# Two half-width subtractions for each low half on GpSimd, and two clears moved to the start of VectorE's program

## What is computed

```
h = rms_norm(x) ; z = h @ w_in                          # first block, 2304 columns
mix = concat(gmlp(z), rglru(z), hgrn2(z), pool(z))       # 256 columns each
x = x + mix @ w_out
x = x + (gelu(conv(hf_gate)) * conv(hf_val)) @ w_down    # hf = rms_norm(x) @ w_up
x = x + (p @ w_pe) * sigmoid(rms_norm(x) @ w_pg)
for l in range(2):                                       # second block
    proj = rms_norm(x) * norm1_g @ w_in
    o_a, o_b, o_c = attention(proj), rwkv7(proj), retention(proj)
    x = x + (g0 * (o_a @ w_attn_o) + g1 * (o_b @ w_rwkv_o) + g2 * (o_c @ w_ret_o)) @ w_out
    x = x + (silu(h2 @ w_ffn_gate) * (h2 @ w_ffn_up)) @ w_ffn_down
```

## Time and profile before

| quantity | value |
|---|---|
| median of three runs | 2712.03 us |
| the profiled execution | 2712.35 us, its span 2710.5 us |
| TensorE (PE) busy | 2621.4 us, 97% of the span |
| VectorE (DVE) busy | 1472.8 us, 54% |
| ScalarE (ACT) busy | 634.3 us, 23% |
| GpSimd (POOL) busy | 1488.5 us, 55% |
| mean granted TensorE clock | 0.992 of full speed |
| DMA, mean over the span | 82 GB/s |

### The profile page before, as it was taken

How to read it: one execution, slowest core, us unless ns; L and a number is a source line. 1 busy time by engine, 2 the same in 40 slices (tenths; PEclk the granted TensorE clock), 3 DMA queues, 4 the chain that set the end, 5 groups by cost and what they waited for, 6 DMA issues and landing times.

```text
span 2710.5 us, 47585 instructions
## 1 busy us (share of the span) xinstructions
PE 2621.4 (97%) x16458; PEld 2043.1 (75%) x16458; DVE 1472.8 (54%) x2059; ACT 634.3 (23%) x1159; POOL 1488.5 (55%) x945
## 2 busy tenths in 40 slices
PE   7889999999999999999999999999999999999999
PEld 5776888877776677787888887766677777888887
DVE  6776737364556637774342424556647774442434
ACT  2333000023324423441200002234413441200002
POOL 4565565655544444456666666644544456666665
PEclk9999999999999999999999999999999999999999
DMA  4212333323211122223333333311122223233332
GB/s 149 67 43 86 93 93 93 93 87 104 85 56 48 36 93 63 59 74 97 93 93 93 93 94 112 94 48 49 41 91 59 71 71 97 93 93 95 95 96 94
DMA packets 72726, 222.67 MB, mean 82 GB/s; under 512 B 9345, under 2 KB 12545, under 8 KB 72577
## 3 DMA queue, kind: packets, MB, share of 16 engines
q1 hardware_dynamic: 72576, 220.63, 27.0%
HBM read 218.50 MB, written 2.10 MB: 81 GB/s over the span
## 4 chain that ended last, share of the span: by engine, by line
PE 88%; DVE 5%; DVEq 2%; issue 2%; DMA 1%; POOL 1%; ACT 1%; POOLq 1%; ACTq 0%; SPq 0%
PE acc L475 77%; PE bank L475 10%; POOL w_lo L354 1%; DMA raw<-in_w_pg 1%; DVEq L1528 1%; PE bank L1048 0%; DVE rw_bon L1086 0%; DVEq L1618 0%; DVE z_rw L1086 0%; DVE rw_SCB L1086 0%; DVE xg_lo L1168 0%; POOL w_hi L347 0%; DMA x<-in_x 0%; DVE rw_Dl L1086 0%; DVE rw_AR L1086 0%
## 5 line engine op out<-in xcount | busy, mean ns | idle before, releaser
L354 POOL TENSOR_TENSOR w_lo<-raw,w_hi 128x1024 fp32r<-128x1024 f32 (+3 forms) x438 | 966.7, 2207 | 303.5 <-PE acc L475 282.3
L347 POOL TENSOR_SCALAR w_hi<-raw 128x1024 fp32r<-128x1024 f32 (+3 forms) x438 | 431.1, 984 | 715.8 <-PE acc L475 607.8
L475 PE MATMUL acc<-xg_hi,w_hi 128*128 128x512 f32 x2224 | 597.5, 406 | 35.7 <-issue 16.2
L475 PE MATMUL acc<-xg_lo,w_hi 128*128 128x512 f32 x2224 | 590.9, 401 | 0.0
L475 PE MATMUL acc<-xg_hi,w_lo 128*128 128x512 f32 x2224 | 588.0, 399 | 0.0
L475 PEld LDWEIGHTS acc<-xg_hi,w_hi 128*128 128x128 f32 x2224 | 414.1, 190 | 153.9 <-issue 60.3
L475 PEld LDWEIGHTS acc<-xg_lo,w_hi 128*128 128x128 f32 x2224 | 418.7, 190 | 105.5 <-issue 5.8
L475 PEld LDWEIGHTS acc<-xg_hi,w_lo 128*128 128x128 f32 x2224 | 416.8, 188 | 101.1 <-issue 0.3
L1895 ACT ACTIVATE ffn_act<-ffn_t 128x512 f32<-128x512 f32 x100 | 63.2, 632 | 778.0 <-DVEq L1146 619.5
L1086 DVE TENSOR_TENSOR x<-x,acc 128x512 f32<-128x512 f32 x104 | 71.3, 689 | 316.1 <-PE acc L475 315.4
L475 PE MATMUL acc<-hid_hi,w_hi 128*128 128x512 f32 x656 | 182.7, 396 | 3.8 <-POOL w_lo L354 1.6
(11 more groups left out here) (342 smaller groups left out, 2835.6 us busy)
## 6 DMA issues: line engine op xcount, KB each, us to landing
raw<-in_w_up SPq DMA_DIRECT2D x132, 512.0 KB, 3.6
raw<-in_w_down SPq DMA_DIRECT2D x48, 512.0 KB, 3.6
raw<-in_w_gate SPq DMA_DIRECT2D x48, 512.0 KB, 3.6
raw<-in_w_ret SPq DMA_DIRECT2D x32, 512.0 KB, 3.6
raw<-in_w_rw SPq DMA_DIRECT2D x28, 512.0 KB, 3.6
raw<-in_w_o SPq DMA_DIRECT2D x48, 256.0 KB, 2.7
raw<-in_w_in SPq DMA_DIRECT2D x18, 512.0 KB, 3.6
raw<-in_w_down SPq DMA_DIRECT2D x24, 384.0 KB, 3.0
```

The lines of the kernel that those rows point to most:

```text
L347: nc.gpsimd.tensor_scalar(w_hi[:, s, 0:n], raw[:, s, 0:n], 1.0, 0.0, ALU.mult, ALU.add).then_inc(w_half[s], 1)
L354: nc.gpsimd.tensor_tensor(w_lo[:, s, 0:n], raw[:, s, 0:n], bits(w_hi[:, s, 0:n]), ALU.subtract).then_inc(w_split[s], 1)
L475: return nc.tensor.matmul(o, a, b, start=first, stop=last, skip_group_check=shared)
```

## The change

Each `low_part` is written as two subtractions of half the columns, one behind the other without a drain between them; the semaphore `w_split` is set by the second. The two clears of VectorE are written ahead of the wait for the first constants (`keep_in`), behind the clear of `sumsq`.

```diff
@@ low_part
-                nc.gpsimd.tensor_tensor(w_lo[:, s, 0:n], raw[:, s, 0:n], bits(w_hi[:, s, 0:n]),
-                                        ALU.subtract).then_inc(w_split[s], 1)
+                for at in (slice(0, n // 2), slice(n // 2, n)):
+                    last = nc.gpsimd.tensor_tensor(w_lo[:, s, at], raw[:, s, at], bits(w_hi[:, s, at]), ALU.subtract)
+                last.then_inc(w_split[s], 1)
@@ start of VectorE's program
             dve.sem_inc(s3["rev"], 1)
             ms(sumsq[:])
+            ms(m1["td"][:])
+            ms(att[:])
             dve.wait_ge(keep_in, load_wait * (len(KEEP) - 1))
@@ behind norm_end(1)
             norm_end(1)
-            ms(m1["td"][:])
-            ms(att[:])
             dve.wait_ge(first_in, load_wait * len(FIRST))
```

## The result

The changed kernel takes 2721.97 us (median of 6 runs, 2716.03 to 2723.58), the kernel before 2712.07 (6 runs beside it, 2710.15 to 2714.28). The ratio is 1.0033, with a 95% interval of 1.0023 to 1.0044. By the bound of 0.2% that is slower, by 9.9 us in the medians and 8.9 us by the ratio. The forecast was 2717.2, and "no change" was given more chance than "slower". The median lies 0.5 us above the upper end of the range (2721.5); by the ratio the time would be 2721.0, and in a second batch the same kernel took 2720.28 (5 runs, ratio 1.0033 again), both just inside it.

The account below looks back on a forecast made before the run. TensorE, busy for 97% of the span, was taken to bound the kernel. Terms of 3.3, 0.75, 0.75, 0.9 and -0.5 summed to +5.2 us, giving 2717.2 us as median; range 2713.0 to 2721.5 us.

Parts of the forecast that it names:

- The price of a subtraction: Every low part on GpSimd: one more subtraction costs 0.15 us, with ends of nothing and 0.35 us.
- Rivals 2 and 4: 2: second half prepared under the first, 2712.6 us, chance 0.12; 4: issue gap between halves, 2724.8 us, chance 0.08.
- Term a: Branch projections and attention part of each layer: TensorE waits for the low part at 22 places, +3.3 us.
- the part on VectorE: Halves reaching TensorE over VectorE: +0.9 us in the recurrence, -0.5 us at 148 us, 0 from 30 to 45 us.
- Term b: Gated embedding: four low parts of slot 0 in a row and one holding up `xg_lo`, +0.75 us.
- Term d: Recurrence, six of eight head pairs: `rw_bon` meets the second half and waits 0.15 us longer, +0.9 us.
- Term e: At 148 us: `m_tc` starts about 0.5 us earlier behind the shorter first half, and this is kept, -0.5 us.
- The zero for 30 to 45 us: First block before TensorE's 4.11 us wait: nothing gained from halves, put at 0, with ends -1 and +0.5 us.
- term c: Four single low parts on the chain and one inside GpSimd's pooling at 172 to 187 us, +0.75 us.
- Rival 1: At `rw_bon` and the convolution: VectorE's waits are halved and this is kept, 2713.0 us, chance 0.15.
- Rival 3: Before 260 us: VectorE's runs pass ahead of GpSimd's second halves, TensorE waits less, 2706.5 us, chance 0.05.

Follow-up runs that it names:

- e6: Kernel before with low parts in quarters everywhere but in the first block's mixers, clears at their old place: 2733.49 us (ratio 1.0081).
- e7: Kernel before with halves only in the layers' attention input pairs and branch projections, clears as before: 2712.97 us (ratio 1.0005).
- e2: Kernel before with halved low parts everywhere, the clears at their old place: 2721.63 us (ratio 1.0030).
- e12: Kernel before with clears moved, halves in first nine input and each layer's first 11 branch pairs, two first-block GpSimd multiplies halved: 2708.55 us (0.9988).
- e9: Kernel before with halves only in the loops that end a layer (output pairs and feed-forward), clears as before: 2710.71 us (ratio 0.9996).
- e4: Kernel before with halved low parts everywhere but in the first block's mixers, clears at their old place: 2717.25 us (ratio 1.0014).

## Why the prediction was right and where it was wrong

**The price of a subtraction** was right: 0.14 us (8.88 for 8.75 in the branch projections, 0.41 for three more in e6), the forecast 0.15. A pair of halves alone took 2.54 to 2.55 us. Rivals 2 and 4 are out by this. (The forecast's own range is a small slip: 38 places by 0.12 to 0.18 us, less 0.5, and one microsecond on either side give 2715.1 to 2719.4, not 2715.3 to 2719.0.)

**Term a, 22 places, +3.3 us**, had the right places and the right price: +1.6 in each layer from 1137 on. What failed is the part on VectorE, which let the change reach TensorE over VectorE only in the recurrence, at 148 and before 45 us. I looked for VectorE's waits where the chain showed them. `an_k` and `an_mx`, 1.70 and 1.20 us in the trace of before, stood in none of my views, and they give 0.9 us back in each layer. With them the 22 places are worth 1.4 us (e7: 0.8).

**Term b, 5 places of the gated embedding, +0.75 us:** the high parts of the circle start at 645.04 and, three rounds on, 667.84 us before, at 644.92 and 668.28 in the changed kernel: 7.79 us for each round instead of 7.60, with 0.15 forecast. The +0.87 of the whole stretch from 575 to 679 us says less, since profiles without a change there have -1.7 to +0.4. Right.

**Term d, `rw_bon`, +0.9 us:** it takes 1.62 us instead of 1.47, as forecast, at the six head pairs named, and from the second head pair to the fourth it is 105.8 us instead of 105.4 in both layers, 0.2 us for each. Right.

**Term e, -0.5 us at 148,** was wrong in sign. I moved `m_tc` against the half of the low part and forgot that GpSimd's next instruction moves too: it was earlier, it was whole, and `m_tc` met it. The zero for 30 to 45 us was too small a gain in most executions: TensorE's wait there, said to grow to 4.4 us, was 1.05 and 1.13 us in the two profiles of the whole change and 3.67 in e2. At 141 us the whole change was 6.7 and 7.4 us ahead, e2 2.2, counted from their first high part. By 250 us nothing of it can be told: -1.3, +0.1 and +2.5 us, where programs unchanged there have -1.8 to +0.1. The part of term c before 250 us lies inside this and was not measured apart.

**What the sum had not at all** is GpSimd's late start at layer 2, 0.9 to 1.3 us once, and the clock: a mean granted clock lower by 0.001 in the medians, with 1 to 3 us. At equal clock the forecast of +5.2 is met by +6 to 8, and in part by luck: a gain of 1.8 in attention, term e's missing 0.5 and the late start nearly cancel. One to three microseconds of the 6 to 8 have no place in this account; the profiles scatter too much between 192 and 1049 us to name one. The clock then took the time to the upper end of the range.

**The rivals.** Rival 1, VectorE's waits shortened and this kept, is what happens in the attention stretch, there with a change of order, and not at `rw_bon`. Rival 3, faster, is what happens up to 141 us: VectorE's run is served ahead of the second halves. I gave it a quarter of 24 us; that much came (6.7 and 7.4 us, not in e2), and was given back at 150 and 188, where GpSimd's own whole instructions and its pooling were next. Its sign, TensorE's waits before 260 us falling by over 5 us together, did not come: 4.11, 3.21 and 2.32 us became 1.05, 6.04 and 6.45. It decided from a point I had not named, whether GpSimd's chain behind is shorter than VectorE's.

## What to carry to other kernels

Splitting an instruction of GpSimd changes when VectorE gets its turn and costs a fixed 0.14 us: split it only where VectorE stands behind it on TensorE's path (here e12's places), and leave it whole where TensorE waits for GpSimd itself. List VectorE's instructions that take longer than their kind by group and form before summing, since the chain of waits shows only the last one. When an engine comes free earlier, ask what it starts next, and read a lead as gained only behind the next place where another engine is late. Before a step between two profiles is put down to a change, look for it in a profile whose program is unchanged up to there.

## What the runs showed of the hardware

- A wait of TensorE can cost more than its length, and not evenly: behind the same 2.35 us wait at the start of the recurrence eight small matmuls took 1.13 us in eight of the profiles and 2.0 in six. Behind the wait at 683 us the half pace lasted 2.1 us longer in the changed kernel and in e9 than in the kernel before, though e9 has the same program there.
- The three series with halves everywhere had a mean granted clock of 0.9902 to 0.9904, the ten others 0.9909 (e4) to 0.9920, over 5 to 11 runs each. Why the whole is lower than its parts stays open.
- GpSimd fetches code at a loop's jump back in some of the programs: 2 packets and a start 0.9 to 1.3 us later in the five with halves or quarters in all parts of the layer loop, neither in the nine others.
- VectorE's small instructions pay the same price as large ones: an `an_mx` of four columns took 1.20 us when it came 0.11 us behind the start of GpSimd's low part, and 0.16 when it came 0.04 us ahead of it.
